# Hymba layer on one core: values from unscaled tokens, norm weight in the weights' split, tokens rescaled during the second value group

## The reference, cut to what matters

```python
h = rmsnorm(x, norm_w)        # x * rsqrt(mean(x^2) + eps) * norm_w; x is 512 x 2048
proj = h @ w_in               # 2048 x 7184: gq gk gv gg glr | hq hf hi hg
log_a = log_sigmoid(glr @ gla_w_up + gla_b_up) / 16      # glr has 16 columns
o_a = chunked_gated_linear_attention(gq, gk, gv, log_a)  # 4 heads
o_b = chunked_gated_linear_attention(hq, 1 - f, hi, log(f))   # 8 heads, f from hf
mixed = concat(head_rmsnorm(o_a) * silu(gg), head_rmsnorm(o_b) * silu(hg))
out = rmsnorm(x + mixed @ w_out, final_norm_w)
```

## Time and profile before

| | |
|---|---|
| median of 3 runs | 865.1 us (865.01 to 865.16) |
| profiled execution | 865.03 us, span 863.3 us |
| PE, PEld busy | 852.0 us (99%), 698.8 us (81%) |
| DVE busy | 591.0 us (68%) |
| ACT busy | 423.2 us (49%) |
| POOL busy | 85.2 us (10%) |
| HBM read, written | 158.56 MB, 58.72 MB |

### The profile page before, as it was taken

How to read it: one execution, slowest core, us unless ns; L and a number is a source line. 1 busy time by engine, 2 the same in 40 slices (tenths; PEclk the granted TensorE clock), 3 DMA queues, 4 the chain that set the end, 5 groups by cost and what they waited for, 6 DMA issues and landing times.

```text
span 863.3 us, 13759 instructions
## 1 busy us (share of the span) xinstructions
PE 852.0 (99%) x5365; PEld 698.8 (81%) x5365; DVE 591.0 (68%) x949; ACT 423.2 (49%) x594; POOL 85.2 (10%) x128
## 2 busy tenths in 40 slices
PE   8999999999999999999999999999999999999996
PEld 5887888888888788888888878888888888888885
DVE  6733476653587747577887978889885669556766
ACT  7521532324455425264465665855655455435454
POOL 4110111110000001011111110000111100000000
PEclk9999999999999999999999999999999999999998
DMA  8276679989654855568776655555777977965554
GB/s 336 66 263 199 173 198 232 197 196 245 224 191 138 275 173 183 184 169 172 153 177 138 157 169 180 150 174 156 163 168 156 279 168 267 346 199 193 195 171 195
DMA packets 75459, 167.75 MB, mean 194 GB/s; under 512 B 7365, under 2 KB 15593, under 8 KB 74505
## 3 DMA queue, kind: packets, MB, share of 16 engines
q1 hardware_dynamic: 45554, 108.02, 37.9%
q0 software_dynamic: 16896, 50.34, 27.4%
q10 hardware_dynamic: 12952, 8.61, 3.4%
HBM read 158.56 MB, written 58.72 MB: 252 GB/s over the span
## 4 chain that ended last, share of the span: by engine, by line
PE 90%; DVE 5%; ACT 2%; issue 1%; DMA 1%; ACTq 0%; DVEq 0%
PE main L577 57%; PE main L837 8%; PE main L773 5%; PE sc L837 4%; PE sc L630 2%; PE st L837 2%; PE po L837 2%; PE po L658 2%; PE st L643 1%; PE sc L773 1%; PE po L661 1%; DVE w_lo L1296 1%; PE main L689 1%; DMA raw<-in_w_in 1%; PE st L773 1%
## 5 line engine op out<-in xcount | busy, mean ns | idle before, releaser
L577 PE MATMUL main<-h_hi,w_hi 128*128 128x512 f32 x640 | 254.2, 397 | 0.1
L577 PE MATMUL main<-h_hi,w_lo 128*128 128x512 f32 x640 | 249.7, 390 | 0.0
L577 PE MATMUL main<-h_lo,w_hi 128*128 128x512 f32 x640 | 249.3, 390 | 0.0
L1296 DVE TENSOR_TENSOR w_lo<-raw,w_hi 128x1024 fp32r<-128x1024 f32 x100 | 122.1, 1221 | 118.6 <-ACT w_hi L885 118.2
L885 ACT ACTIVATE w_hi<-raw 128x1024 fp32r<-128x1024 f32 x100 | 105.6, 1057 | 188.8 <-PE main L577 132.2
L577 PEld LDWEIGHTS main<-h_hi,w_lo 128*128 128x128 f32 x640 | 120.1, 188 | 25.8
L577 PEld LDWEIGHTS main<-h_hi,w_hi 128*128 128x128 f32 x640 | 120.2, 188 | 25.5 <-issue 0.5
L577 PEld LDWEIGHTS main<-h_lo,w_hi 128*128 128x128 f32 x640 | 120.3, 188 | 23.7
L907 ACT ACTIVATE ex<-ex 128x512 f32<-128x512 f32 (+2 forms) x84 | 52.0, 640 | 21.4 <-DVE ex L1434 14.7
L577 PE MATMUL main<-w_hi,h_hi 128*128 128x512 f32 x128 | 51.4, 402 | 0.0
L577 PE MATMUL main<-w_lo,h_hi 128*128 128x512 f32 x128 | 50.5, 394 | 0.0
(11 more groups left out here) (314 smaller groups left out, 1496.5 us busy)
## 6 DMA issues: line engine op xcount, KB each, us to landing
raw<-in_w_in SPq DMA_DIRECT2D x102, 512.0 KB, 4.6
w_sum<-in_w_out POOLq DMA_DIRECT2D x48, 512.0 KB, 5.2
w_sum<-in_w_in POOLq DMA_DIRECT2D x24, 512.0 KB, 5.6
w_sum<-w_sum POOLq DMA_DIRECT2D x24, 512.0 KB, 6.2
raw<-w_sum SPq DMA_DIRECT2D x24, 512.0 KB, 4.2
feat<-w_sum SPq DMA_DIRECT2D x24, 512.0 KB, 4.1
raw<-in_w_out SPq DMA_DIRECT2D x14, 512.0 KB, 4.7
feat<-in_w_out SPq DMA_DIRECT2D x10, 512.0 KB, 4.7
```

What stands on the lines that cost most here:

```text
L577: mm = pe.matmul(main[c][:, :], a, b, start=(k == 0 and j == 0), stop=(k == KT - 1 and j == 2))
L1296: dve.tensor_tensor(w_lo[:, q % SPL, :, :], (first_raw if first else raw)[:, q % RAW, :, :], w_hi[:, q % SPL, :, :], ALU.subtract).then_in ...
```

## The change

It takes the norm out of the path to the value products. The tokens are transposed as they come, unscaled; SP loads x by column groups of 512 (x_first, x_second, x_in), and PE walks the opening by column groups with tokens inside. The norm weight, transposed to one number per partition and k tile (nwp), is applied where the weights of groups 0 and 1 are split: ACT and DVE do each piece as two instructions with nwp as scale. The root comes in with the value copies (tensor_scalar with rs). For glr, lr_raw is multiplied by nwp, and the result by the row of roots, which PE broadcasts from a diagonal (rstd_rows); the ACT copies then wait for lr_tok.

From the queries on, the tokens are needed scaled. POOL adds h_hi and h_lo back together into feat (unsplit), DVE multiplies by nwp and the row (scale_tokens, two instructions a piece), ACT rounds again (scaled_high) and DVE takes the rest (scaled_low). Pieces 0 to 3 of this run during group 1, the rest in G_A, where PE waits for h_ok before each piece. The Strassen sums start two pieces later. The diff, cut to its core:

```diff
-TURNED = [(0, 0), (1, 0), (0, 1), (2, 0), (3, 0), (1, 1), (2, 1), (3, 1)]
-NORMALISED = [(0, 0), (1, 0), (0, 1), (2, 0), (1, 1), (3, 0), (2, 1), (3, 1)]
-
-
 def turned(t, j):
 
-    return 2 * TURNED.index((t, j // 2)) + j % 2 + 1
+    return NT * j + t + 1
...
+        row = feat[:, 16, :]
+        diag = feat[:, 17, :]
+        lr_tmp = feat[0:2 * LOWRANK, 18, :]
+        nwp = feat[:, 19, 0:KT]
+        nw16 = feat[0:KT, 19, P:2 * P]
...
-            x_halves(0)
-            group(w_in, C_GV, G_V, range(0, 3))
-            x_halves(1)
-            group(w_in, C_GV, G_V, range(3, 4))
-            x_tile(2)
-            x_tile(3)
...
+            sp.dma_start(nw16, norm_w.rearrange("(k p) -> k p", p=P)).then_inc(nw_in, 16)
+
+            def x_columns(t, q, n, ready):
+                cols = slice(q * GW, (q + n) * GW)
+                sp.dma_start(xin[:, t, cols], x[t * P:(t + 1) * P, cols]).then_inc(ready[t], 16)
+
+            x_columns(0, 0, 1, x_first)
+            group(w_in, C_GV, G_V, range(0, 2))
+            for t in range(1, NT):
+                x_columns(t, 0, 1, x_first)
+            group(w_in, C_GV, G_V, range(2, 4))
+            for t in range(NT):
+                x_columns(t, 1, 1, x_second)
+            for t in range(NT):
+                x_columns(t, 2, 2, x_in)
...
+            def unsplit(p):
+
+                ks = slice(p * PK, (p + 1) * PK)
+                if p == 0:
+                    pool.wait_ge(xt_lo, KT)
+                    pool.wait_ge(xss, NT)
+                pool.tensor_tensor(feat[:, ks, :], h_hi[:, ks, :], h_lo[:, ks, :], ALU.add).then_inc(hx_ok, 1)
+
             for pair in (2, 0, 1):
                 if pair == 0:
                     paced[0] = D_N + ND
                 for j, (name, source) in enumerate(COPIED):
                     for q in range(QP):
                         pace()
+                        if pair == 2 and NP <= QP * j + q < 2 * NP:
+                            unsplit(QP * j + q - NP)
...
+            def first_products():
+
+                ts = slice(0, P)
+                pe.wait_ge(xt_hi, 1)
+                pe.wait_ge(hi_ok, 1)
+                for kk in range(PK):
+                    pe.matmul(main[0][:, :], h_hi[:, kk, ts], w_hi[:, 0, kk, :], start=(kk == 0), stop=False)
+                pe.wait_ge(lo_ok, 1)
+                for kk in range(PK):
+                    pe.matmul(main[0][:, :], h_hi[:, kk, ts], w_lo[:, 0, kk, :], start=False, stop=False)
+                pe.wait_ge(xt_lo, 1)
+                for kk in range(PK):
+                    pe.matmul(main[0][:, :], h_lo[:, kk, ts], w_hi[:, 0, kk, :], start=False, stop=False)
+
+            def rstd_rows():
+
+                pe.wait_ge(row_in, 1)
+                pe.matmul(st[:, :], ones, diag, start=True, stop=True).then_inc(row_ps, 1)
...
+            filler(2)
+            pe.wait_ge(nw_in, 16)
+            pe.transpose(st[:, 0:KT], nw16, ident[0:KT, 0:KT]).then_inc(nb_ps, 1)
+            filler(3)
             transposes(0, 0)
-            filler(2)
-            opening(0, (0, 1, 2))
-            transposes(1, 0)
-            opening(0, (3,))
-            opening(1, (0, 1))
-            transposes(0, 1)
-            opening(1, (2,))
-            transposes(2, 0)
-            opening(1, (3,))
-            opening(2, (0, 1))
-            transposes(3, 0)
-            transposes(1, 1)
-            opening(2, (2, 3))
-            transposes(2, 1)
-            opening(3, (0, 1))
-            transposes(3, 1)
-            opening(3, (2, 3))
-            pe.wait_ge(xt_lo, KT)
-            group(0, True, {31: [parameters]}, range(HP, NP))
+            filler(3)
+            for n in range(KT):
+                t, j = n % NT, n // NT
+                if n == 0:
+                    first_products()
+                else:
+                    opening(t, 2 * j)
+                for m in ((1, 2) if n == 0 else (n + 2,)):
+                    if m < KT:
+                        transposes(m % NT, m // NT)
+                    if m == 1:
+                        opening(t, 1)
+                if n:
+                    opening(t, 2 * j + 1)
+                if n == 9:
+                    rstd_rows()
+            pe.wait_ge(nb_ok, 1)
+            parameters()
             group(1, True, {8: [low_rank], 16: [decay_inputs]})
-            group(G_A, False)
+            group(G_A, False, before=lambda p: pe.wait_ge(h_ok, p + 1))
...
+                src = (first_raw if first else raw)[:, q % RAW, :, :]
+                if isinstance(G, int) and G * NP + q < 2 * NP:
+                    for kk in range(PK):
+                        k = (q % NP) * PK + kk
+                        mm = act.activation(w_hi[:, q % SPL, kk, :], src[:, kk, :], ACT.Copy, scale=nwp[:, k:k + 1])
+                    mm.then_inc(hi_ok, 1)
...
+            highs(0, 0)
+            act.wait_ge(nb_ok, 1)
             split(0, -3)
             split(0, -2)
-            highs(0, [0, 1])
+            highs(1, 0)
             split(0, -1)
-            half_squares(1)
+            highs(2, 0)
             split(0, 0)
-            highs(1, [0, 1])
+            highs(3, 0)
+            highs(0, 1)
+            squares(0)
+            highs(1, 1)
+            squares(1)
+            highs(2, 1)
+            split(0, 1)
             squares(2)
+            highs(3, 1)
+            split(0, 2)
             squares(3)
+            highs(0, 2)
...
+                act.wait_ge(lr_tok, 1)
...
+            def scaled_high(p):
+                def f():
+                    act.wait_ge(hs_ok, p + 1)
+                    act.wait_ge(piece_done, NP + max(p + 1, 3))
+                    act.wait_ge(lr_ps, 1)
+                    ks = slice(p * PK, (p + 1) * PK)
+                    act.activation(h_hi[:, ks, :], feat[:, ks, :], ACT.Copy).then_inc(hr_hi, 1)
+                return f
+
+            group(0, {}, lambda c: None, 5)
             group(1, {0: [bounds], 1: [values_out(0, 0)], 2: [values_out(0, 1)], 3: [low_rank, values_out(0, 2)],
-                      4: [values_out(0, 3)], 5: [decays]}, lambda c: None)
+                      4: [values_out(0, 3), scaled_high(0)], 5: [decays, scaled_high(1)], 6: [scaled_high(2)],
+                      7: [scaled_high(3)]}, lambda c: None)
...
+                        mm = dve.scalar_tensor_tensor(out=w_lo[:, q % SPL, kk, :], in0=src[:, kk, :],
+                                                      scalar=nwp[:, k:k + 1], in1=w_hi[:, q % SPL, kk, :],
+                                                      op0=ALU.mult, op1=ALU.subtract)
+                    mm.then_inc(lo_ok, 1)
...
+            lows(0, 0)
             split(0, -3)
-            lows(0, [0])
             split(0, -2)
-            lows(0, [1])
+            lows(1, 0)
             split(0, -1)
-            norm_row(3)
-            normalise(1, 0)
+            lows(2, 0)
             split(0, 0)
-            lows(1, [0, 1])
-            dve.wait_ge(nb_ok, 4)
-            normalise(0, 1)
-            normalise(2, 0)
-            normalise(1, 1)
-            lows(0, [2, 3])
-            lows(2, [0, 1])
-            normalise(3, 0)
-            normalise(2, 1)
-            normalise(3, 1)
-            lows(3, [0, 1])
-            lows(1, [2, 3])
-            lows(2, [2, 3])
+            lows(3, 0)
+            for t in range(3):
+                lows(t, 1)
             split(0, 1)
-            lows(3, [2, 3])
+            lows(3, 1)
+            split(0, 2)
+            lows(0, 2)
...
+                    dve.tensor_scalar(val[:, c, half * GW:(half + 1) * GW], main[c][:, :], rs[:, c:c + 1], None,
+                                      ALU.mult).then_inc(free[c], 1)
+                return f
+
+            group(0, {}, values(0), 5, NP - 1)
...
+                dve.wait_ge(lr_ps, 1)
+                dve.wait_ge(row_ok, 1)
+                step(dve.tensor_tensor(lr_tmp, st[0:n, :], row[0:n, :], ALU.mult))
+                dve.sem_inc(lr_tok, 1)
...
+            def scale_tokens(p):
+                def f():
+                    dve.wait_ge(hx_ok, p + 1)
+                    for k in range(p * PK, (p + 1) * PK):
+                        mm = dve.scalar_tensor_tensor(out=feat[:, k, :], in0=feat[:, k, :], scalar=nwp[:, k:k + 1],
+                                                      in1=row, op0=ALU.mult, op1=ALU.mult)
+                    mm.then_inc(hs_ok, 1)
+                return f
+
+            def scaled_low(p):
+                def f():
+                    dve.wait_ge(hr_hi, p + 1)
+                    ks = slice(p * PK, (p + 1) * PK)
+                    dve.tensor_tensor(h_lo[:, ks, :], feat[:, ks, :], h_hi[:, ks, :], ALU.subtract).then_inc(h_ok, 1)
+                return f
+
+            group(1, {3: [low_rank, scale_tokens(0)], 4: [scale_tokens(1), scaled_low(0)],
+                      5: [decays, scale_tokens(2), scaled_low(1)], 6: [scale_tokens(3), scaled_low(2)],
+                      7: [scale_tokens(4), scaled_low(3)]}, values(1))
...
```

(53 more changed lines are left out.)

135 lines of the change are left out of this document (45 added, 90 removed).

## The result

The changed kernel took 881.12 us (median of 5, 880.55 to 881.9) against 865.1 (864.56 to 865.32): ratio 1.0185, 95% interval 1.0174 to 1.0196. It is slower, as forecast, but by 16.0 us where I had 6.0, and outside my range.

A forecast was written before the change was run, and what follows sets the result against it. TensorE's work queue was taken to bound the kernel, so only its start and new stalls count. Opening -2.9, low rank +0.8, value copies +6.5, clock +1.6 sum to +6.0 us on 865.1: 871.1 us, range 867.0 to 876.0.

The forecast's parts named there:

- Sign and place: Slower, chance 0.86, with the main stall on TensorE before the first query product, waiting for a value copy on VectorE.
- part 3: Second group's value copies: 7.4 us of rescaling ahead of them on VectorE, less 0.95 slack, stalls the queries 6.5 us.
- Contention: GpSimd's eight additions beside VectorE: GpSimd pays, with several microseconds before each user, so the sum takes nothing.
- Rival B: VectorE also pays for contention during decays and catch-up: +3 to +6 us on the stall, about 875.5; chance 0.20.
- Rival D: The opening's gain is eaten by an unseen wait, time near 873.5 us; chance 0.05.
- The opening: Start to second value group: first product at 7.5 us, second group at 61.5 for 64.39; gain 2.9 us (1.5 to 3.8).
- no wait ends late: Opening's rounds on TensorE: every awaited input is ready in time, so no wait takes from the gain.
- The low rank: Decay inputs in the second value group: ScalarE's copies wait for lr_tok from VectorE; cost 0.8 us (0.4 to 1.3).
- The clock: TensorE's stop before the queries drops the clock, so they start at 1.2 GHz; cost 1.6 us (0 to 3).
- No further stall: After the value copies: 4 to 6 us of VectorE work per 5.45 us piece, h_ok four pieces ahead, no wait.

The follow-up runs named there:

- experiment 5: Changed kernel with the second group's value copies ahead of scale_tokens 2 to 4 and scaled_low 1 to 3, additions unmoved: 871.08 us, ratio 1.0065.
- experiment 1: Changed kernel without GpSimd's eight additions (unsplit only gives its semaphore; output not the layer's): 875.02 us, ratio 1.0111.
- experiment 8: Changed kernel, additions waiting for VectorE gaps, value copies before rescaling, low rank earlier; first group's copies of banks 0, 1 before splits: 870.54 us; behind: 873.44.
- experiment 9: Changed kernel with the rescaling left out whole, low rank and first group's copies moved earlier (output not the layer's): 863.53 us, ratio 0.9978.
- experiment 4: Changed kernel with the eight additions moved earlier, four in a row behind the 9th piece and four behind the 10th: 887.51 us, ratio 1.0257.
- experiment 2: Kernel before with only GpSimd's eight additions put in, into tiles nothing reads, and ScalarE's query and key copies waiting for them: 867.23 us, ratio 1.0023.

## Why the prediction was right and wrong, point by point

**Sign and place: right.** The queries waited for value copy 0 on VectorE behind scale_tokens 2 to 4 and scaled_low 1 to 3, without a gap from the decays to the copies, as part 3 said. Experiment 5 shows that this order is worth 10 us in the changed kernel, and experiment 1 that its queueing alone is 6.7 us of wait for a forecast of 6.5.

**Contention: wrong, and the largest error.** The step that failed is the term for the contention, which the sum takes at nothing: "Where GpSimd ran beside VectorE, GpSimd paid". I had read that off one row, two tiny casts that took 1.32 us beside a VectorE instruction of unchanged length. That row shows GpSimd coming second. With an exclusion the one that comes second waits, and a row in which the short one comes second says nothing of the case in which the 2.4 us one comes first. I gave the case in which VectorE pays a chance of 0.20 and +3 to +6 us. The Trainium skill's page "GPSIMD Engine Reference" (section Key points) names contention for the shared SBUF interfaces between just this pair of instructions, and the rows above agree; by its table an addition was estimated at 2.2 us, where 2.40 were measured. What the contention cost: 6.1 us in all (experiment 1), 4.3 of them on the value copies' wait and 1.6 on that of the decay inputs. Rival B had the mechanism and, at its upper end, nearly the size, but not the sum, since the other terms were off too: without the additions the kernel still took 875.02 us, 3.9 above my forecast of 871.1. (Rival D's 873.5 should read 874.0, the forecast plus 2.9; nothing hangs on it.)

**The opening: right in kind, mis-sized.** First product 7.93 for 7.5. PE was through with the first group at 62.5 us (63.97 less the wait of 1.51) in place of 61.5, a gain of 1.9: the fast pace began at about 13.5 and not 12 (matmuls 0.43 us apart until then), and the splits of a piece took 1.34 us on ScalarE where I had 1.2. Then a wait of 1.5 us that I had called absent: "no wait ends late" covered the way to round 15 only. Value copy 0 of the first group stands on VectorE behind the splits of pieces 8 and 9, and these behind ScalarE's low-rank weights and a table load, to 59.05. I had checked the copies' due time for the second group and not for the first. Experiment 8 (the pair) shows that this order costs at least the 1.5 us seen (2.9 between the medians); experiment 9 that some 1.7 us is what the opening brings in the end.

**The low rank: right, and held.** Without the additions the decay inputs waited 0.8 us, the forecast to the digit; with them 2.4, since two of the chain's steps lay beside an addition.

**The clock: right.** It fell to 0.50, and the restart cost 1.6 to 2.0 us for a forecast of 1.6. I had drawn it from the end of the kernel, where PE stops and the clock follows some 3 us later.

**"No further stall": right as run, for the wrong reason.** In the changed kernel nothing waits after 130 us that is new beyond 0.6 us (a kd, L1495). But with the queries on time the keys wait: 1.6 us in experiment 5, 5.0 in experiment 8; in both, six steps of rescaling precede the queries' first split. That the late start of the queries hid this wait in the changed kernel is my reading; no run isolates it. My statement that 4 to 6 us of VectorE work fit into 5.45 us a piece left no room for such a row of steps, nor for the weight loads behind that split.

## What to carry to other kernels

When work is added to an engine, list for every buffer that this engine hands back the step at which it does so, first group and second alike, and count the new steps that stand ahead of it: here the same steps of rescaling cost 10 us more ahead of four copies than behind them. An idle GpSimd is not free capacity beside a busy VectorE: price each of its SBUF instructions at up to its own full length on VectorE, place it where VectorE has a gap or slack, and be wary of several in a row (experiment 4). And when a stall goes, look at once for the next one, since the stall may have been giving the later chain its slack.

## What the runs showed of the hardware that I had not expected

A GpSimd addition of 128x1024 took 2.40 us, a copy some 1.05. A VectorE instruction with two SBUF tensors that came while either ran behaved as if it did not start before: it ended 1.09 us (1024 elements) or 0.55 (512) behind GpSimd's end, and even one of 8 elements ended only with it (69.30, 2.19 us for 0.17). The exclusion goes both ways (GpSimd's 2.40 became 2.92, its 1.05 became 1.60). It held for a subtraction from SBUF, a scalar_tensor_tensor, the tiny ones and, in the one row that shows it, a one-input tensor_scalar from SBUF to SBUF (1.03 for 0.43); one-input instructions that read PSUM kept their length (0.75 at 107.92; 2.48 for four copies in experiment 2). With four additions in a row, a VectorE instruction of 0.17 us once stood for 9.74 us until the last was through, and in another row of four got a turn after each; what decides between the two was not shown.
